# Two feed-forwards of a transformer kernel computed by Strassen's scheme

## The reference, cut to what matters

```
def conv_ffn(x, w_in, conv_w, conv_b, w_out):
    a, b = jnp.split(x @ w_in, 2, axis=-1)          # w_in 1024 x 5632
    a_pad = jnp.pad(a, ((0, 0), (CONV_W - 1, 0), (0, 0)))
    a = sum(conv_w[k] * a_pad[:, k:k + S] for k in range(CONV_W)) + conv_b
    return (jax.nn.gelu(a) * b) @ w_out             # w_out 2816 x 1024
...
x = layer_norm(ALPHA * x + mix, ln1_g[layer], ln1_b[layer])
ffn = conv_ffn(x, ...)
x = layer_norm(ALPHA * x + ffn, ln2_g[layer], ln2_b[layer])
```

## Time and profile before

| | us |
|---|---|
| median of 3 runs | 1548.4 |
| the profiled execution | 1543.75 |
| its span | 1542.0 |
| TensorE busy | 1307.4 |
| VectorE busy | 330.1 |
| ScalarE busy | 255.3 |
| GpSimd busy | 72.7 |
| feed-forward of layer 0, from its first product | 917.7 to 1145.2 |
| feed-forward of layer 1 | 1300.9 to 1528.3 |

### The profile page before, as it was taken

How to read it: one execution, slowest core, us unless ns; L and a number is a source line. 1 busy time by engine, 2 the same in 40 slices (tenths; PEclk the granted TensorE clock), 3 DMA queues, 4 the chain that set the end, 5 groups by cost and what they waited for, 6 DMA issues and landing times.

```text
span 1542.0 us, 15877 instructions
## 1 busy us (share of the span) xinstructions
PE 1307.4 (85%) x6479; PEld 816.7 (53%) x6479; DVE 330.1 (21%) x793; ACT 255.3 (17%) x635; POOL 72.7 (5%) x123
## 2 busy tenths in 40 slices
PE   7999989766566656657997799999999989999996
PEld 6864544312212212213775568777767745877774
DVE  3332524101101100102016431111130143111114
ACT  4312421000000000002025511000020241100000
POOL 4000100000000000000003200000000120000000
PEclk9999889987888878889998999999999989999998
DMA  9612126999999999999433029443444404344300
GB/s 313 215 55 109 55 85 235 412 421 421 422 422 422 422 422 422 422 421 401 147 110 110 1 72 337 164 163 136 162 165 137 164 1 137 109 164 163 136 0 28
DMA packets 112740, 335.46 MB, mean 218 GB/s; under 512 B 6617, under 2 KB 58129, under 8 KB 88110
## 3 DMA queue, kind: packets, MB, share of 16 engines
q1 hardware_dynamic: 110070, 326.33, 55.3%
q0 software_dynamic: 2416, 8.30, 1.6%
q10 hardware_dynamic: 199, 0.06, 0.0%
HBM read 333.59 MB, written 2.86 MB: 218 GB/s over the span
## 4 chain that ended last, share of the span: by engine, by line
PE 65%; DMA 24%; DVE 6%; ACT 3%; issue 1%; SPq 1%; DVEq 0%; ACTq 0%
PE bank L729 43%; DMA ring<-in_w_expert_up 22%; PE bank L1043 9%; PE bank L1077 5%; DMA ring<-in_a_w_in 1%; PE bank L1302 1%; PE bank L875 1%; PE bank L1351 1%; DVE small L2394 1%; ACT arena L1784 1%; SPq L626 1%; PE bank L1274 1%; ACT wide_rows L1663 1%; ACT arena L1793 1%; PE bank L906 1%
## 5 line engine op out<-in xcount | busy, mean ns | idle before, releaser
L729 PE MATMUL bank<-wide_rows,ring 128*128 128x256 f32 (+2 forms) x2080 | 460.6, 381 | 5.0 <-DMA ring<-in_a_w_in 2.4
L729 PEld LDWEIGHTS bank<-wide_rows,ring 128*128 128x128 f32 (+1 forms) x2080 | 396.3, 193 | 74.2 <-issue 17.7
L1077 PE MATMUL bank<-ring,arena 128*32 128x512 f32 x992 | 153.0, 773 | 130.7 <-DMA ring<-in_w_expert_up 123.3
L729 PE MATMUL bank<-ring,wide_rows 128*128 128x512 f32 (+3 forms) x416 | 172.8, 574 | 1.2 <-DVE wide_rows L2414 1.1
L1077 PEld LDWEIGHTS bank<-ring,arena 128*32 128x32 f32 x992 | 40.7, 137 | 240.4 <-issue 224.4
L1043 PE MATMUL bank<-ring,arena 128*128 128x512 f32 x352 | 154.3, 592 | 0.0
L729 PEld LDWEIGHTS bank<-ring,wide_rows 128*128 128x128 f32 (+1 forms) x416 | 77.1, 188 | 87.0 <-issue 84.2
L1043 PEld LDWEIGHTS bank<-ring,arena 128*128 128x128 f32 x352 | 66.9, 190 | 75.7 <-issue 74.6
L2491 DVE SCALAR_TENSOR_TENSOR arena<-bank,cols,arena 128x255 f32<-128x255 f32 x44 | 21.2, 483 | 341.4 <-ACT arena L1820 341.4
L1820 ACT ACTIVATE arena<-bank,cols 128x256 f32<-128x256 f32 x44 | 24.8, 564 | 372.2 <-PE bank L729 372.2
L2228 DVE TENSOR_TENSOR arena<-arena,bank 64x512 f32<-64x512 f32 x16 | 11.1, 691 | 316.0 <-ACT arena L1678 316.0
(11 more groups left out here) (313 smaller groups left out, 953.2 us busy)
## 6 DMA issues: line engine op xcount, KB each, us to landing
ring<-in_w_expert_down SPq DMA_DIRECT2D x32, 2048.0 KB, 24.9
...
ring<-in_ffn_w_in SPq DMA_DIRECT2D x44, 1024.0 KB, 10.4
...
```

Source lines behind the costliest of these rows:

```text
L729: last = pe.matmul(dst, lhsT, rhs, start=k == 0, stop=k == len(pairs) - 1)
L1077: last = pe.matmul(bank[e % 2][at:at + SLOTS, :], xg_tile(e % 2, k)[:, SLOTS * r:SLOTS * r + SLOTS], w[r][:, kk, :], start=k == 0, stop=k ...
```

## The change: what it does, and the diff

Both matrix products of each feed-forward are computed by the Winograd form of Strassen's scheme on 2 x 2 blocks: 7 block products in place of 8, with sums of blocks before and after.

Up: the rows are split into two blocks of 128, the features into two halves of 512, and the output columns into a and b. For each of the 22 tiles of 128 hidden columns TensorE does 7 block products of 4 k-tiles, each with 128 moving columns; the first and second share an accumulator. GpSimd forms four sums of the weights per tile (each 128 x 512), VectorE four sums of the row columns once per layer. The results stand in two banks; ScalarE copies the first out and VectorE forms a and b from them by five sums in SBUF; the taps now read from there. Four pairs of banks take turns. The product of the first blocks (first_columns) of tiles 0 and 1 is done before the second row block is turned, that of tiles 2 and 3 right after.

Down comes after all of up, and its hidden columns are kept in SBUF. For each of 11 pairs of hidden tiles TensorE does 7 products of 512 columns into seven banks. GpSimd forms four sums of the output weights per pair (VectorE for the last pair), VectorE four sums of the hidden blocks. The last three pairs are done product by product, so that a bank is complete after each three, and VectorE adds the banks into the rows while the next ones run. The ring takes all 11 input units first and then the 6 output units. The loops are unrolled, and the products on zeros around the feed-forwards go. GpSimd's load of the gain and bias vectors moves behind its fifth set of weight sums.

```diff
+QUARTER = 4 * P
+LAST_PAIRS = (STEPS_F - 3, STEPS_F - 2, STEPS_F - 1)
...
-for j in range(0, STEPS_F - 1, 2):
-  order.extend([(f"ffn_in{layer}", j), (f"ffn_in{layer}", j + 1), (f"ffn_out{layer}", j // 2)])
-order.extend([(f"ffn_in{layer}", STEPS_F - 1), (f"ffn_out{layer}", STEPS_F // 2)])
+order.extend([(f"ffn_in{layer}", j) for j in range(STEPS_F)] + [(f"ffn_out{layer}", j) for j in range((STEPS_F + 1) // 2)])
...
+hidden_F = take(FFT * T, FFT, T)
+at_sums = used[0]
+w_sums = [take(4 * QUARTER, 4, QUARTER) for _ in range(2)] + [view(at_hb, 4 * QUARTER, 4, QUARTER)]
+ab = [take(4 * P) for _ in range(3)]
+x_sums = R[:, :, :].rearrange("p a (b n) -> p (a b) n", n=QUARTER)
+h_sums = [mem_kv[:, i].rearrange("p a b -> p (a b)").rearrange("p (s t) -> p s t", t=P) for i in (0, 2)] + [
+  ab[1].rearrange("p (s t) -> p s t", t=P)]
...
+up_banks = [(bank[4], bank[5]), (bank[6], bank[7]), (bank[0], bank[1]), (bank[2], bank[3])]
+down_banks = {1: bank[0], 2: bank[1], 3: bank[2], 6: bank[3], 5: bank[4], 7: bank[5], 4: bank[6]}
...
+def down_sums(p):
+  return w_sums[2 if p == STEPS_F - 1 else p % 2]
+def hidden_sums(p):
+  return h_sums[2 if p == STEPS_F - 1 else p % 2]
+def weights_landed(engine, layer, what, j):
+  n = ffn_at(layer, what, j)
+  engine.wait_ge(landed[n % RING], use_count(n))
...
+      ph = phase_sems["ffn" + what[-1]]
+      if 2 * c + 1 < LAST_PAIRS[0]:
+        sp.wait_ge(ph["used"], 2 * c + 2)
+      else:
+        sp.wait_ge(ph["first"], 7)
...
+  def ffn(layer, name, ahead):
+    def up_sums(u, i, at, weights, columns):
+      for k in range(KT // 2):
+        last = pe.matmul(up_banks[u % 4][i][:, at * P:(at + 1) * P], weights(k), columns(k), start=k == 0, stop=k == KT // 2 - 1)
+      return last
+    def turned(j, tb):
+      return lambda k: XT[:, KT // 2 * j + k, tb * P:(tb + 1) * P]
+    def as_loaded(u, h, j):
+      w = up_weights(layer, u)[h][j]
+      return lambda k: w[:, k, :]
+    def summed(rows, i):
+      return lambda k: rows[:, i, k * P:(k + 1) * P]
+    def first_columns(u, j):
+      weights_landed(pe, layer, "in", u // 2)
+      up_sums(u, j, 0, as_loaded(u, 0, j), turned(j, 0))
+    def up(u):
+      s = w_sums[u % 2]
+      if u >= 4:
+        pe.wait_ge(ph["summed"], u - 3)
+        first_columns(u, 0)
+        first_columns(u, 1)
+      pe.wait_ge(ph["w_sums"], 4 * u + 1)
+      if u == 0:
+        pe.wait_ge(ph["x_sums"], 1)
+      up_sums(u, 0, 2, summed(s, 0), summed(x_sums, 0))
+      pe.wait_ge(ph["w_sums"], 4 * u + 2)
+      if u == 0:
+        pe.wait_ge(ph["x_sums"], 2)
+      up_sums(u, 0, 3, summed(s, 1), summed(x_sums, 1))
+      pe.wait_ge(ph["w_sums"], 4 * u + 3)
+      if u == 0:
+        pe.wait_ge(ph["x_sums"], 3)
+      up_sums(u, 0, 1, summed(s, 2), summed(x_sums, 2))
+      if u == 0:
+        pe.wait_ge(ph["x_sums"], 4)
+      up_sums(u, 1, 2, as_loaded(u, 1, 1), summed(x_sums, 3))
+      pe.wait_ge(ph["w_sums"], 4 * u + 4)
+      up_sums(u, 1, 1, summed(s, 3), turned(1, 1)).then_inc(ph["tile"], 1)
+    def down(p, which):
+      b, hs, ws = down_weights(layer, p), hidden_sums(p), down_sums(p)
+      block = lambda j, tb: hidden_F[:, 2 * p + j, tb * P:(tb + 1) * P]
+      left, right = {1: (block(0, 0), b[0][0]), 2: (block(1, 0), b[1][0]), 3: (hs[:, 3, :], b[1][1]),
+             4: (block(1, 1), ws[:, 3, :]), 5: (hs[:, 0, :], ws[:, 0, :]), 6: (hs[:, 2, :], ws[:, 2, :]),
+             7: (hs[:, 1, :], ws[:, 1, :])}[which]
+      return pe.matmul(down_banks[which][:, :], left, right, start=p == 0, stop=p == STEPS_F - 1)
+    def sums_of(p, n):
+      pe.wait_ge(ph["w_sums"], 4 * FFT + 4 * p + n)
+    pe.wait_ge(normed, ahead + 1)
+    for j in range(2):
+      transposes(name, j, [((P, r * P, P), X[:, 0, (4 * j + r) * P:(4 * j + r + 1) * P]) for r in range(4)])
+    for what, part in between(name, 0):
+      mem_product(what, part)
+    for j in range(2):
+      wait_emptied(pe, name, j)
+      for u in range(2):
+        first_columns(u, j)
+    pe.wait_ge(normed, ahead + 2)
+    for j in range(2):
+      transposes(*((name + "_last", 0) if j == 1 else (name, 2)), [((P, r * P, P), X[:, 1, (4 * j + r) * P:(4 * j + r + 1) * P]) for r in range(4)])
+    for what, part in between(name, 1):
+      mem_product(what, part)
+    wait_emptied(pe, name, 2)
+    wait_emptied(pe, name + "_last")
+    for what, part in between(name, 1):
+      wait_emptied(pe, what, part)
+    for u in range(2, 4):
+      for j in range(2):
+        first_columns(u, j)
+    for u in range(FFT):
+      up(u)
+    pe.wait_ge(ph["summed"], FFT - 2)
+    for p in range(LAST_PAIRS[0]):
+      if p % 2 == 0:
+        weights_landed(pe, layer, "out", p // 2)
+      pe.wait_ge(ph["hidden"], 2 * p + 2)
+      down(p, 1)
+      down(p, 2)
+      pe.wait_ge(ph["h_sums"], p + 1)
+      down(p, 3)
+      if p == 0:
+        pe.wait_ge(ph["summed"], FFT)
+      for n, which in enumerate((5, 7, 6, 4)):
+        sums_of(p, n + 1)
+        last = down(p, which)
+      last.then_inc(ph["used"], 1)
+    weights_landed(pe, layer, "out", LAST_PAIRS[0] // 2)
+    weights_landed(pe, layer, "out", LAST_PAIRS[-1] // 2)
+    pe.wait_ge(ph["hidden"], FFT)
+    pe.wait_ge(ph["h_sums"], STEPS_F)
+    pe.wait_ge(ph["x_sums"], 8)
+    for which in (1, 6, 5, 2, 3, 7, 4):
+      for p in LAST_PAIRS:
+        if which == 6 and p < STEPS_F - 1:
+          sums_of(p, 3)
+        elif which == 4 and p < STEPS_F - 1:
+          sums_of(p, 4)
+        last = down(p, which)
+      last.then_inc(ph["first"], 1)
+  ffn(0, "xTf0", 2)
...
+    def keep_first(u):
+      act.wait_ge(ph["tile"], u + 1)
+      if u >= 3:
+        act.wait_ge(ph["hidden"], u - 2)
+      act.activation(ab[u % 3][:, 0:P], up_banks[u % 4][0][:, 0:P], ACT.Copy).then_inc(ph["kept"], 1)
+    def tap(u):
+      act.wait_ge(ph["summed"], u + 1)
+      act.activation(hidden_F[:, u, :], ab[u % 3][:, 0:T], ACT.Identity, scale=cols[:, at_w + 2 * FFT + u:at_w + 2 * FFT + u + 1],
+             bias=cols[:, at_b + u:at_b + u + 1]).then_inc(ph["act"], 1)
+    def gelu(u):
+      act.wait_ge(mulp[f"ffn{layer}"], u + 1)
+      act.activation(hidden_F[:, u, :], hidden_F[:, u, :], ACT.Gelu_apprx_tanh).then_inc(act2[f"ffn{layer}"], 1)
+    for u in range(FFT + 2):
+      if u < FFT:
+        keep_first(u)
+      if 1 <= u < FFT + 1:
+        tap(u - 1)
+      if u >= 2:
+        gelu(u - 2)
+    act.wait_ge(ph["first"], 1)
+    act.activation(ab[0], down_banks[1][:, :], ACT.Copy).then_inc(ph["kept"], 1)
...
+      if (tb, n) == (0, 0):
+        dve.wait_ge(phase_sems[name]["kept"], FFT + 1)
+        stt(rows(0, 0), rows(0, 0), ALPHA, product(1), ALU.mult, ALU.add)
+        dve.wait_ge(first, 2)
+        step(tt(u2, u2, product(6), ALU.add))
+        stt(rows(0, 1), rows(0, 1), ALPHA, u2, ALU.mult, ALU.add)
+        step(stt(both, both, ALPHA, halves(u2), ALU.mult, ALU.add))
+        dve.wait_ge(first, 3)
+        tt(rows(0, 1), rows(0, 1), product(5), ALU.add)
+        tt(rows(1, 1), rows(1, 1), product(5), ALU.add)
+        dve.wait_ge(first, 4)
+        step(tt(rows(0, 0), rows(0, 0), product(2), ALU.add))
+      elif (tb, n) == (0, 1):
+        dve.wait_ge(first, 5)
+        step(tt(rows(0, 1), rows(0, 1), product(3), ALU.add))
+      elif (tb, n) == (1, 0):
+        dve.wait_ge(first, 6)
+        step(tt(both, both, halves(product(7)), ALU.add))
+        dve.wait_ge(first, 7)
+        step(tt(rows(1, 0), rows(1, 0), product(4), ALU.add))
...
+    def summed(u):
+      (x, y), r = up_banks[u % 4], ab[u % 3]
+      twos = lambda v: v.rearrange("p (a b) -> p a b", b=P)
+      dve.wait_ge(ph["kept"], u + 1)
+      step(tt(r[:, 3 * P:4 * P], r[:, 0:P], x[:, P:2 * P], ALU.add))
+      step(tt(twos(r[:, P:3 * P]), twos(x[:, 2 * P:4 * P]), r[:, 3 * P:4 * P].unsqueeze(1).broadcast_to([P, 2, P]), ALU.add))
+      tt(r[:, 3 * P:4 * P], r[:, 2 * P:3 * P], x[:, 2 * P:3 * P], ALU.add)
+      step(tt(r[:, 0:P], r[:, 0:P], y[:, 0:P], ALU.add))
+      tt(r[:, P:3 * P], r[:, P:3 * P], y[:, P:3 * P], ALU.add).then_inc(ph["summed"], 1)
+    def conv(u):
+      tap = lambda t: cols[:, at_w + t * FFT + u:at_w + t * FFT + u + 1]
+      w, a = hidden_F[:, u, :], ab[u % 3]
+      dve.wait_ge(ph["act"], u + 1)
+      stt(w[:, 1:T], a[:, 0:T - 1], tap(1), w[:, 1:T], ALU.mult, ALU.add).then_inc(conv1[name], 1)
+      dve.wait_ge(conv1[name], u + 1)
+      stt(w[:, 2:T], a[:, 0:T - 2], tap(0), w[:, 2:T], ALU.mult, ALU.add).then_inc(mulp[name], 1)
+    def gate(u):
+      dve.wait_ge(act2[name], u + 1)
+      tt(hidden_F[:, u, :], hidden_F[:, u, :], ab[u % 3][:, 2 * P:4 * P], ALU.mult).then_inc(ph["hidden"], 1)
+    def hidden_summed(p):
+      s = hidden_sums(p)
+      block = lambda j, tb: hidden_F[:, 2 * p + j, tb * P:(tb + 1) * P]
+      dve.wait_ge(ph["hidden"], 2 * p + 2)
+      if 2 <= p < STEPS_F - 1:
+        dve.wait_ge(ph["used"], p - 1)
+      step(tt(s[:, 0, :], block(0, 1), block(1, 1), ALU.add))
+      tt(s[:, 1, :], block(0, 0), block(0, 1), ALU.subtract)
```

(117 more changed lines are left out.)

104 lines of the change are left out of this document (31 added, 73 removed).

## The result

The changed kernel takes **1524.65 us** (median of 4 runs, 1521.13 to 1526.29) against 1548.24 (4 runs, 1543.4 to 1548.67) of the kernel before on the same chip: a ratio of 0.9857, 95% interval 0.9836 to 0.9879. Forecast were 1525 and a range of 1505 to 1543. The profiled execution took 1524.56 us with a span of 1522.8.

The account below looks back on a forecast made before the run. TensorE was taken as the bound, 85% busy. Terms -47.0 + 7.9 + 1.8 - 1.3 + 4 + 15.2 - 3.8 = -23.2 took the profiled 1543.75 to 1520.5; the median's 4.65 offset gave 1525 us, range 1505 to 1543.

Parts of the forecast that it names:

- The products: TensorE's up and down products: 6.27 us per up tile, 0.86 saved per down pair; 23.5 us saved a feed-forward, 47.0 both.
- rival 3: Weight loads exposed in long product streams: above 120 ns a record all gain is gone, at 193 1725 us; chance 0.03.
- VectorE beside GpSimd in the up stage: Per up tile, VectorE takes 5.7 us with waits and GpSimd 5.3, both covered by TensorE's 6.27; no cost.
- turns: VectorE and GpSimd alternate, each waiting for the other's whole instruction; VectorE sums reading one PSUM operand are spared.
- Rival 2: Shared access of VectorE and GpSimd paces the up stage: 7.5 us a tile, +44, 1569 us; chance 0.10.
- Start of layer 0: Before tiles 2 and 3, TensorE waits for the second input weight unit: +7.9 us, and +1.8 for lost clock.
- Start of layer 1: First columns of tiles 0 and 1 run before the second block is turned: -1.3 us (-4 to +2).
- From up to down: First down step waits for the last tile's sums: 2 us stall (0.3 to 5), +4 for both layers.
- Entry to the last three pairs: TensorE waits for VectorE's hidden sums alternating with GpSimd: 5.8 us plus 1.8 clock a layer, +15.2 for both.
- Tails: Behind TensorE's last product, 2.3 us remain in layer 0 and 4.0 in layer 1: -1.5 and -2.3 us.
- the stalls at their dear ends: Upper end of the range: forecast with every stall at its dear end (5, 8, 11 and 3.5), said to add 16.

Follow-up runs that it names:

- experiment 5: Changed kernel with the first GpSimd sum of every up tile and down pair made a multiplication, read for durations alone; 1521.14 us (one run).
- Experiment 1: Changed kernel with layer 0's up(0) and up(1) run before the first columns of tiles 2 and 3; 1513.34 us, ratio to the kernel before 0.9806.
- experiment 2: Changed kernel with an own buffer for pair 9's hidden sums, so they need not wait for down(7); 1522.65 us, ratio to the kernel before 0.9845.
- Experiment 6: Changed kernel with VectorE's four weight sums of the last pair split, two behind pair 5 and two behind pair 6; 1518.26 us (one run).
- Experiments 3: Changed kernel with GpSimd's weight sums of pair 9 held until VectorE's hidden sums are all done; 1513.55 us (one run).
- 4: Changed kernel with 28 products of zeros ahead of the wait for the last hidden sums; 1521.55 us (one run).
- experiment 7: Changed kernel with the edits of experiments 1, 2, 3 and 6 plus twelve zero products before layer 1's first wait; 1496.87 us, ratio to before 0.9693.

## Why the prediction was right, and where only the sum was

- **The products: right.** 6.25 us a tile (forecast 6.27), 6.00 a pair (before 6.87), so 22 x 0.65 + 11 x 0.86 = 23.8 a layer against 23.5. The start-to-start distance of the earlier trace rows held over 56 records of every tile; the 192 ns of a load stayed hidden, and rival 3 is out. By an estimate from the Trainium skill's page "TensorE: Matmul & The Clock Gate", section "Back-to-back issue gap" (81 ns with loads where the products alone take 56), loads would have spaced these products nearly half as wide again. The trace, 111.6 ns against half of 215.8, does not agree for fp32.
- **VectorE beside GpSimd in the up stage: right, with one price wrong.** The step "GpSimd adds four 128x512 sums per tile: 4 x 1.04" was mis-sized: alone they take 1.26 each, with turns 1.30 to 1.38. The 5.3 us a tile that the forecast reached by adding 3 x 0.3 for turns is what was measured, but by luck: the turns were put as much too dear as the sums too cheap. The prediction had read the 1.26 of L2578 in the earlier trace rows as a slowed 1.04; it is the shortest time of experiment 5's sums and products too. VectorE's convolution steps take 1.05 and 1.38, the gate 1.34; with the five sums from PSUM (0.28 to 0.42, undisturbed) that is 5.5 us busy a tile, against the 5.7 forecast. Both stay under 6.25, with less than 1 us left each. Rival 2 did not come, but it was near.
- **Start of layer 0: right.** 8.52 us of idling for the input weights, then 32 records in 5.27 us in place of 3.58 at half clock. From the first transposes to the tiles' regular pace, less the 7.2 us of first columns, it is 19.0 against 10.5: +8.6 where stall and clock were put at 9.7. Experiment 1 made layer 0 9.8 us shorter: the 8.52 and the 1.69 of clock went, and 0.63 of a new wait came.
- **Start of layer 1: wrong sign, small.** The same count gives 15.2 - 7.2 = 8.1 against 7.6: +0.5, not -1.3. The parenthesis of that step had it (the filler products that go might cost clock): 2.69 us of idling, then half clock for part of the 32 records. In experiments 1, 2 and 6, whose edits leave this start alone, the clock stayed up behind the same idling and the count gives 6.4, that is -1.2, the forecast; the sign hangs on the clock alone.
- **From up to down: wrong place.** Forecast 2 us a layer, measured 0. VectorE had the last tile's sums ready in time. In its stead 1.33 us were lost in pair 6 of each layer, which no step named: the four weight sums of the last pair (0.68, 1.75, 1.75 and 1.64 us, in turn with GpSimd) stand ahead of pair 6's hidden sums. Experiment 6 shows it: with two of the four moved, the wait is gone.
- **Entry to the last three pairs: right in kind, a little short.** Forecast a wait of 5.8 and 1.8 for the clock; measured 6.46 in both layers, and 2.7 and 1.6. The term 4 x 1.04 is the short one again: GpSimd's four sums took 1.31 to 1.40 each, 5.4 together. Experiments 3 and 4 show the two parts separately. My later idea that the shared buffer was most of it failed in experiment 2; the prediction's own account, turns, was the better one.
- **Tails: right.** The second statistics end 2.1 us after TensorE's last product of layer 0 (forecast 2.3) and 3.7 after that of layer 1 (forecast 4.0).

By layer, the forecast was -23.5 + 9.7 + 2 + 7.6 - 1.5 = -5.7 and -23.5 - 1.3 + 2 + 7.6 - 2.3 = -17.5; measured were -5.2 and -15.9. So the size of each layer's gain is right by itself to 1.6 us. That the median fell on the forecast to 0.4 us is partly luck, as the part ahead of layer 0 scatters by 4 us either way. The forecast was -23.2 from one profiled execution to the next, where the two spans differ by 19.2; the rest is that the execution profiled before was 4.65 us under its median and the one after was not. One sum of the range does not come out: the stalls at their dear ends add 11.6 us by the terms given, not 16 (14.9 with the dear end of layer 1's start), which would end the range near 1537 to 1540; the result lies inside by either.

One reading the forecast should have made from its own terms: the down half, as given, brings nothing but its shorter tails. It saves 11 x 0.86 = 9.5 us a layer and pays 6.46 + 2.7 + 1.3 = 10.5 in layer 0 and 9.4 in layer 1; the tails give 1.8 and 2.7. Most of the gain is the up half's. This is a count on one trace, since no run has the up half alone; but experiment 7 leaves 1.5 to 1.7 us a layer of those costs, which is where some 16 of its further 28 us come from; 9.8 more are the start of layer 0.
